# Low parts of fourteen weight units made by accumulating DMAs, and one more Strassen row tile pair, in the down projection of a decoder layer

## The reference, cut to what matters

```python
h = rms_norm(x, ln_mix_w)                      # token mixer, two branches, gates
x = x + merged @ w_out
u = causal_depthwise_conv(rms_norm(x, ln_ffn_w) @ w_up, conv_w, conv_b)
u_gate, u_val = jnp.split(u, 2, axis=-1)
x = x + (jax.nn.silu(u_gate) * u_val) @ w_down     # the down projection: 5504 -> 2048
x = x + jax.nn.sigmoid(rms_norm(x, ln_ple_w) @ w_ple_gate) * (p @ w_ple)
return rms_norm(x, ln_final_w)
```

## Time and profile before

| | |
|---|---|
| runs | 1428.85 us median of 3 (1428.69 to 1429.17) |
| profiled execution, span | 1427.1 us |
| the median above the span | 1.75 us |
| TensorE busy | 1417.3 us, 99% of the span |
| VectorE, ScalarE, GpSimd busy | 1072.4, 786.4 and 152.7 us |
| DMA, share of 16 engines | 59.7% for the loads' queue |

### The profile page before, as it was taken

How to read it: one execution, slowest core, us unless ns; L and a number is a source line. 1 busy time by engine, 2 the same in 40 slices (tenths; PEclk the granted TensorE clock), 3 DMA queues, 4 the chain that set the end, 5 groups by cost and what they waited for, 6 DMA issues and landing times.

```text
span 1427.1 us, 19876 instructions
## 1 busy us (share of the span) xinstructions
PE 1417.3 (99%) x7076; PEld 1204.1 (84%) x7076; DVE 1072.4 (75%) x1366; ACT 786.4 (55%) x955; POOL 152.7 (11%) x103
## 2 busy tenths in 40 slices
PE   9999999999999999999999999999999999999997
PEld 7888888888888888888888888888888888888886
DVE  7676777878687878777777777777777888888755
ACT  7555655545455555565555555555555555555544
POOL 0044144100000000000111101101011000000000
PEclk9999999999999999999999999999999999999999
DMA  9655555455755675566656666566665556565653
GB/s 324 199 175 164 155 172 171 145 188 163 232 190 179 212 247 196 168 211 182 198 170 201 183 191 194 173 199 186 191 194 179 200 198 200 170 213 199 232 200 121
DMA packets 190877, 273.48 MB, mean 192 GB/s; under 512 B 11744, under 2 KB 103136, under 8 KB 190688
## 3 DMA queue, kind: packets, MB, share of 16 engines
q1 hardware_dynamic: 190384, 272.30, 59.7%
q10 hardware_dynamic: 432, 0.37, 0.1%
HBM read 270.53 MB, written 2.10 MB: 191 GB/s over the span
## 4 chain that ended last, share of the span: by engine, by line
PE 98%; DVE 1%; issue 0%; DMA 0%; ACT 0%; SPq 0%; ACTq 0%; POOLq 0%; POOL 0%; DVEq 0%
PE aux L915 11%; PE main L915 11%; PE main L700 10%; PE main L701 10%; PE main L702 10%; PE aux L924 6%; PE main L924 6%; PE main L758 5%; PE main L760 5%; PE main L759 5%; PE aux L758 3%; PE aux L760 3%; PE aux L759 3%; PE aux L702 2%; PE aux L700 2%; PE aux L701 2%
## 5 line engine op out<-in xcount | busy, mean ns | idle before, releaser
L1523 DVE TENSOR_TENSOR w_lo<-raw,w_hi 128x1024 fp32r<-128x1024 f32 (+1 forms) x478 | 587.7, 1241 | 291.8 <-ACT w_hi L1208 291.1
L1208 ACT ACTIVATE w_hi<-raw 128x1024 fp32r<-128x1024 f32 (+1 forms) x478 | 502.1, 1052 | 469.6 <-PE main L702 133.8
L700 PE MATMUL main<-w_hi,xT 128*128 128x512 f32 x510 | 201.5, 395 | 0.4 <-DVE w_lo L2032 0.3
L701 PE MATMUL main<-w_lo,xT 128*128 128x512 f32 x510 | 198.6, 389 | 0.0
L702 PE MATMUL main<-w_hi,xT 128*128 128x512 f32 x510 | 198.6, 389 | 0.0
L915 PE MATMUL aux<-xT,w_hi 128*128 128x512 f32 x704 | 169.7, 391 | 0.0
L915 PE MATMUL main<-xT,w_hi 128*128 128x512 f32 x672 | 162.8, 391 | 0.0
L915 PEld LDWEIGHTS aux<-xT,w_hi 128*128 128x128 f32 x704 | 129.4, 188 | 25.0
L915 PEld LDWEIGHTS main<-xT,w_hi 128*128 128x128 f32 x672 | 123.2, 188 | 23.6
L2140 POOL TENSOR_TENSOR act<-cv 128x512 f32<-128x512 f32 (+1 forms) x22 | 71.9, 3267 | 418.5 <-DVE cv L1747 418.5
L700 PEld LDWEIGHTS main<-w_hi,xT 128*128 128x128 f32 x510 | 95.8, 188 | 20.2 <-DVE xT L1550 1.2
(11 more groups left out here) (334 smaller groups left out, 2180.6 us busy)
## 6 DMA issues: line engine op xcount, KB each, us to landing
raw<-in_w_up SPq DMA_DIRECT2D x336, 256.0 KB
raw<-in_w_in SPq DMA_DIRECT2D x136, 512.0 KB
raw<-in_w_down SPq DMA_DIRECT2D x84, 512.0 KB
raw<-in_w_out SPq DMA_DIRECT2D x32, 512.0 KB
raw<-in_w_ple_gate SPq DMA_DIRECT2D x32, 512.0 KB
raw<-in_w_branch_a SPq DMA_DIRECT2D x16, 512.0 KB
raw<-in_w_branch_b SPq DMA_DIRECT2D x16, 512.0 KB
raw<-in_w_in SPq DMA_DIRECT2D x15, 256.0 KB, 5.7
```

Source lines behind the costliest of these rows:

```text
L700: pe.matmul(acc, th, wh, start=first, stop=False)
L701: pe.matmul(acc, th, wl, start=False, stop=False)
L1208: ac.activation(w_hi[:, u % RING, :, 0:w], raw[:, u % RING, :, 0:w], ACT.Copy).then_inc(hi_full, 1)
L1523: dve.tensor_tensor(w_lo[:, u % RING, :, 0:w], raw[:, u % RING, :, 0:w], w_hi[:, u % RING, :, 0:w].bitcast(F32), ALU.subtract).then_inc(lo ...
```

## The change

Two edits. First, `SEVEN_AT` gives the second half six Strassen pairs, 3, 6, 9, 12, 14 and 17, where it had 5, 8, 11, 14 and 17; the first half keeps its five.

Second, for fourteen units (`LO_BY_DMA`, always the second chunk, a = 1) VectorE no longer makes the low part. ScalarE, right behind the high part, writes minus the rounded raw to `w_lo`, and a DMA from GpSimd's queue adds `raw` to it in place (`accum_op=ALU.add`). The tile pairs are 6, 9, 12, 15 and 18 in the first half, each right behind a Strassen pair, and 4, 5, 7, 8, 10, 11, 13, 16 and 18 in the second. TensorE at the unit, and SP before it loads the slot again, wait for the DMA's landing (`lo_added`, one semaphore for each slot); the count in `lo_full` leaves these units out.

```diff
-SEVEN_AT = ((5, 8, 11, 14, 17), (5, 8, 11, 14, 17))
+SEVEN_AT = ((5, 8, 11, 14, 17), (3, 6, 9, 12, 14, 17))
...
+LO_BY_DMA = [down_unit(p, i, 1) for p, rows in enumerate([(6, 9, 12, 15, 18), (4, 5, 7, 8, 10, 11, 13, 16, 18)]) for i in rows]
+
+
+def lo_split(u):
+
+    return u + 1 - sum(v <= u for v in LO_BY_DMA)
...
+        def lo_arrived(eng, u, it=None):
+
+            if it is None and u in LO_BY_DMA:
+                eng.wait_ge(lo_added[u % RING], 16 * sum(v <= u and v % RING == u % RING for v in LO_BY_DMA))
+            else:
+                eng.wait_ge(lo_full, plus(lo_split(u), 2 * UK, it))
...
                 if u >= RING:
-                    sp.wait_ge(lo_full, plus(u - RING + 1, 2 * UK, it))
+                    lo_arrived(sp, u - RING, it)
...
             def down_plain(u, p, i, a):
 
-                pe.wait_ge(lo_full, u + 1)
+                lo_arrived(pe, u)
...
                 ac.activation(w_hi[:, u % RING, :, 0:w], raw[:, u % RING, :, 0:w], ACT.Copy).then_inc(hi_full, 1)
+                if it is None and u in LO_BY_DMA:
+                    ac.activation(w_lo[:, u % RING, :, :], raw[:, u % RING, :, :], ACT.Copy, scale=-1.0).then_inc(hi_negated, 1)
...
-                if u >= UNITS:
+                if u >= UNITS or (it is None and u in LO_BY_DMA):
                     return
...
+            for k, u in enumerate(LO_BY_DMA):
+                pool.wait_ge(hi_negated, k + 1)
+                pool.dma_start(w_lo[:, u % RING, :, :], raw[:, u % RING, :, :], accum_op=ALU.add).then_inc(lo_added[u % RING], 16)
             root(2)
```

More of the change, by code:

```diff
@@ L355, in build @@
         lo_full = sem("lo_full")
+        hi_negated, lo_added = sem("hi_negated"), [sem(f"lo_added{r}") for r in range(RING)]
         units_done = sem("units_done")
@@ L704, in unit @@
             def unit(u, c, i, n, hi, lo, k, it=None, width=NCOL, tiles=2):
-                pe.wait_ge(lo_full, plus(u + 1, 2 * UK, it))
+                lo_arrived(pe, u, it)
                 for a in range(tiles):
@@ L1168, in _ @@
                 for j in range(SPLIT_TB):
-                    pe.wait_ge(lo_full, u + j + 1)
+                    lo_arrived(pe, u + j)
                     for a in range(2):
@@ L1175, in _ @@
                     main_released(c - 1)
-                pe.wait_ge(lo_full, u + SPLIT_TB + 1)
+                lo_arrived(pe, u + SPLIT_TB)
                 if tb == 0:
```

## The result

| | before | after |
|---|---|---|
| runs, median | 1428.82 us (1428.69 to 1429.17) | 1469.26 us (1465.71 to 1470.57) |
| ratio, 95% interval | | 1.0279 [1.0266, 1.0292] |
| profiled span | 1427.1 us | 1468.8 us |

What follows compares the result with a forecast made beforehand. TensorE, busy 1417.3 of 1427.1 us, was taken to bound the kernel. Ten waits 17.0, four others 1.0, turnover 0.5, matmuls -0.7 gave +17.8 us, so 1446.7 us; range 1428.0 to 1465, likeliest case 1434 to 1465.

Steps and rivals of the forecast that it cites:

- Ten units wait, the allowance is 3.8 us: Down projection, units right behind a Strassen pair: 3.8 us from DMA request to TensorE's need, so 1.7 us wait each, 17.0.
- The DMA takes 5.5 us, bounds 2.8 to 7.6: Accumulating 512 KB DMA, request to landing: priced like a same-size load that finds one transfer ahead of it.
- Of nearly equal length: Sign in the new profile: TensorE's ten DMA waits nearly equal, one cycle of three tile pairs apart (15.6 us plus wait).
- The granted clock is 1.00 there, and I expect no change of it.: Down projection: TensorE's clock stays at the 2.4 GHz level, so nothing was charged for it.
- The four loose units, together 1.0: DMA units at tile pairs 5, 8, 11, 16, with 4.9 us left: wait 0.6 us at most each, together 1.0.
- Turnover +0.5: Start of the second half: crowded VectorE delivers one low part some 0.4 us late, once; taken as 0.5, bounds 0 to 2.5.
- Between 12 and 14 nothing: Closer Strassen pairs of the second half: freed VectorE time stands against the closer sums, so no cost was taken.
- SP's reload charged at nothing: SP's reload of a slot waits for the DMA's landing, some 0.7 us late, but TensorE is already held 1.7; no charge.
- Rival 2: Down projection: DMA as long as a 1024 KB copy or longer; 7.6 us gives +48.6 us, 1477; chance 0.12 beyond 1465.
- Rival 1: Down projection: DMA lands in 2.8 to 4.0 us and fits; time unchanged, -0.2 to +1.8 us, 1428.7 to 1430.7; chance 0.27.
- Rival 4: Down projection: DMA traffic delays the weights, TensorE waits behind ScalarE's high parts instead; 5 to 20 us; chance 0.08.
- rival 3: Down projection: freed VectorE time dissolves load bursts, faster by over 0.2% (2.9 us), though 0.9 us is the ceiling; chance 0.03.

## Why the prediction was wrong, step by step

- **TensorE bounds the kernel, and only an operand past its slack hurts.** Right.
- **Ten units wait, the allowance is 3.8 us.** Right: ten waits at exactly these units, and 3.7 us by nine of them. That TensorE's waiting would not loosen it held too.
- **The DMA takes 5.5 us, bounds 2.8 to 7.6.** This is the step that failed. It measured 4.4 to 8.8, mean 6.5 to TensorE's start: ten times 1.0 above the term, 27.6 us of waits instead of 17.0. The additions landed behind the last load of the burst, not beside it: its last packet ended 5.5 to 5.9 us behind the request in the four long ones, and the addition needs 2.8 more. Single additions ran past the upper bound, and the lower was out of reach (2.8 is a plain copy). The rows for a better value stood there: the earlier trace rows have the third load of the burst asked for at 1134.1 and landed by 1140.56, with the request at 1135.25 behind it. Had I queued the addition behind that load instead of taking the row of one that "finds one ahead of it", the landing would have been 1140.56 plus the addition's own time, 2 x 1.45 = 2.9 us in the experiments' rows: 8.2 after the request. Four of the ten measured 8.3 to 8.8. The 2.9 could not be known from the rows before, which have no addition. The Trainium skill's fit for this path ("DMA: Bandwidth & Descriptors", section on the anatomy of a DMA), an estimate of 3.2 us for 512 KB, lies near the plain copy's least of 2.8; the addition's least of 4.4 and the 8.7 beside loads lie well above it. The Trainium skill's sentence on the same page, that DMAs of all issuing engines run on the same 16 engines and interleave, agrees with the trace: from 1182.5 to 1183.4 us packets of both queues move.
- **Of nearly equal length.** Wrong: 0.7 to 5.0 us, since the end of the burst lies 1.3 to 5.9 us behind the request at nine of the ten places.
- **"The granted clock is 1.00 there, and I expect no change of it."** Wrong, and the second largest error: 11.4 us. Behind each wait of over 4 us the clock was at the 1.2 GHz level for seven to thirteen matmuls, each 0.2 us dearer. Behind those of 0.7 to 1.1 us it was not, and of the three of 2.0 to 2.2 only behind the one of 2.12.
- **The four loose units, together 1.0.** None waited in the changed kernel. For tile pairs 5, 8 and 11 the wait of the tight unit just ahead may give them time; pair 16 has none just ahead, and no run shows why it did not wait. Without tight units they waited 2.7 us in all: 4.5 to 5.0 us less an allowance of 4.1 to 4.3, where the prediction had counted 4.9.
- **Turnover +0.5.** Right in place and about in size: 0.3 and 0.2 us. **Between 12 and 14 nothing:** wrong without the DMAs (1.16 us); in the changed kernel, which has less VectorE work and more waiting, there is no such wait. As a whole the sixth pair costs 1.7 us alone, not the -0.2 of my sum.
- **VectorE's 14 subtractions worth nothing, ScalarE's 14 negations hidden.** Right in the main: 14 rows of 1.04 us more on ScalarE, none of which TensorE waits for by itself (they stand ahead of the request, as the prediction counted). What the subtractions were worth alone no run shows; at most it is the 1.16 us wait that the changed kernel lacks.
- **SP's reload charged at nothing.** Half right. No wait names it, but the hold ties the loads to the landings, and in two stretches of the kernel with the later wait that loop alone sets the pace. This is the main reason that the runs show for later waits and earlier requests bringing some 3 us instead of 20.
- **The rivals.** Rival 2 (dearer DMA) has the size, but by another way: not 7.6 us everywhere, but 6.5 in the mean plus the clock. Rival 1 is out: no addition of the fourteen came under 4.4. Rival 4 (weights late) shows in the kernel that holds a load back (5.3 us) and a little in the one with the later wait (0.95 and 0.56 us), and rival 3 not at all.

The two misses together, 10.6 us of waits and 11.4 of clock, are 22.0 of the 23.9 us between the 17.8 forecast and the 41.7 measured.

## What to carry to other kernels

Price a DMA that is asked for in the middle of a burst as one that ends behind the whole burst, not as a transfer on its own: take the end of the last load ahead of it and add its own engine time (here 2.8 us for an addition of 512 KB, about double that of a copy), and take its time beside idle engines (here 4.4) where that is later. Loads that are asked for behind it can make it later still. When a forecast puts a wait of several microseconds on a TensorE that was busy without a hole, add the clock's part to it. Before lengthening an allowance, follow the wait's own chain back to the same wait one turn earlier: if TensorE isn't in it, time given to TensorE doesn't shorten it.

## What the runs showed of the hardware

- An accumulating DMA of 512 KB from SBUF to SBUF holds the DMA engines for 2.83 us, a plain copy 1.45; from request to landing they take 4.4 and 2.8 us at the least.
- With the last of three 512 KB loads asked for 0.4 to 1.2 us ahead, it takes 8.3 to 8.8 us to TensorE's start, with two ahead 5.5 at the same place, with the third 2.7 us ahead 4.5 to 5.9. At nine of the ten places it landed 2.8 us behind the last packet of these loads, or at 4.4 us.
- The granted clock fell to 0.50 around waits of 4.3 to 5.0 us of a TensorE that had been busy for 15 us and more before but for waits of up to 0.3 us, and came back by itself within 3 to 6 us of work. The length of the wait alone does not decide it: in the kernel that held the third load it was at half behind waits of 2.19 and 2.23 us (starts 0.43 us apart from 1143.74), but at 1.00 behind one of 2.40 (1246.2 to 1250.2), and in the kernel with the later wait at 1.00 behind one of 3.00 (1164.2 to 1168.2). What exactly decides it stays open.
